# Attention of a two-layer decoder: three of four query tiles computed in quarters between the heads, the sample scores as one more unit of the rotation, the output projection begun inside it

## The reference

```
def sink_attention(q, k, v, dist, valid, sinks, rel_bias):
    ...
    s = jnp.einsum('nqgrd,nkgd->ngrqk', q, k, ...) * ATTN_SCALE + bias
    s = jnp.where(valid, s, NEG_INF)
    m = jnp.maximum(jnp.max(s, axis=-1, keepdims=True), sink)
    p = jnp.exp(s - m)
    probs = p / (jnp.sum(p, axis=-1, keepdims=True) + jnp.exp(sink - m))
    return jnp.einsum('ngrqk,nkgd->nqgrd', probs.astype(v.dtype), v)

q = (rmsnorm(x, g_mix[l]) @ w_q[j])
o = window_attn_prompt(...) or window_attn_sample(...)
x = x + o @ w_o[j]
h = rmsnorm(x, g_ffn[l])
x = x + moe_swiglu(h, ...)
```

## Time and profile before

| | |
|---|---|
| median of 3 runs | 1666.62 us (1665.63 to 1669.33) |
| the profiled execution, its own time | 1667.54 us |
| its span | 1665.8 us |
| PE busy | 1541.1 us, 93% |
| PEld busy | 1311.5 us |
| DVE busy | 1228.1 us, 74% |
| ACT busy | 962.3 us, 58% |
| chain that ended last, by engine | PE 89%, DVE 6%, ACT 2% |

### The profile page before, as it was taken

How to read it: one execution, slowest core, us unless ns; L and a number is a source line. 1 busy time by engine, 2 the same in 40 slices (tenths; PEclk the granted TensorE clock), 3 DMA queues, 4 the chain that set the end, 5 groups by cost and what they waited for, 6 DMA issues and landing times.

```text
span 1665.8 us, 22245 instructions
## 1 busy us (share of the span) xinstructions
PE 1541.1 (93%) x8280; PEld 1311.5 (79%) x8281; DVE 1228.1 (74%) x1137; ACT 962.3 (58%) x904; POOL 120.0 (7%) x141
## 2 busy tenths in 40 slices
PE   2589989999889879999998999998999999999995
PEld 1578989999777768888887888887888888888884
DVE  7843565553654257989887889887988988888984
ACT  3433443433454226777765776765776776776772
POOL 3970102000100000000000000000000000000000
PEclk9679989999975679999999999999999999999998
DMA  2004588445440025999987999997999998999980
GB/s 99 26 1 162 202 130 301 180 174 180 149 184 1 11 91 228 359 374 349 368 316 284 369 361 352 363 338 280 359 366 360 358 363 313 355 362 363 359 353 28
DMA packets 61933, 423.56 MB, mean 254 GB/s; under 512 B 8302, under 2 KB 8454, under 8 KB 11665
## 3 DMA queue, kind: packets, MB, share of 16 engines
q1 hardware_dynamic: 58784, 412.37, 65.6%
q0 software_dynamic: 3056, 9.85, 3.0%
HBM read 415.31 MB, written 6.88 MB: 253 GB/s over the span
## 4 chain that ended last, share of the span: by engine, by line
PE 89%; DVE 6%; ACT 2%; issue 2%; DMA 0%; SPq 0%; DVEq 0%; ACTq 0%
PE ps L1633 25%; PE ps L1635 24%; PE ps L1634 24%; PE ps L1828 2%; PE ps L1841 1%; PE ps L1463 1%; PE ps L1521 1%; PE ps L1552 1%; PE ps L1553 1%; PE ps L1854 1%; PE ps L1721 1%; PE ps L1748 1%; PE ps L1499 1%; PE ps L1710 1%; ACT WH L635 1%
## 5 line engine op out<-in xcount | busy, mean ns | idle before, releaser
L1138 DVE TENSOR_TENSOR WL<-raw,WH 128x2048 fp32r<-128x2048 f32 x387 | 885.8, 2292 | 211.7 <-ACT WH L635 208.2
L635 ACT CAST WH<-raw 128x2048 fp32r<-128x2048 f32 x387 | 738.4, 1910 | 201.0 <-PE ps L1635 201.0
L1633 PE MATMUL ps<-WH,XEH 128*128 128x512 f32 x896 | 361.8, 404 | 10.5 <-DVE WL L1138 9.0
L1635 PE MATMUL ps<-WH,XEL 128*128 128x512 f32 x896 | 353.1, 394 | 0.0
L1634 PE MATMUL ps<-WL,XEH 128*128 128x512 f32 x896 | 351.6, 392 | 0.0
L1633 PEld LDWEIGHTS ps<-WH,XEH 128*128 128x128 f32 x896 | 169.4, 189 | 45.6 <-DVE WL L1138 9.4
L1635 PEld LDWEIGHTS ps<-WH,XEL 128*128 128x128 f32 x896 | 169.4, 189 | 42.8
L1634 PEld LDWEIGHTS ps<-WL,XEH 128*128 128x128 f32 x896 | 169.4, 189 | 35.3
L1633 PE MATMUL ps<-WH,AFH 128*128 128x512 f32 x448 | 178.2, 398 | 0.0
L1634 PE MATMUL ps<-WL,AFH 128*128 128x512 f32 x448 | 176.8, 395 | 0.0
L1635 PE MATMUL ps<-WH,AFL 128*128 128x512 f32 x448 | 176.8, 395 | 0.0
(11 more groups left out here) (358 smaller groups left out, 1845.3 us busy)
## 6 DMA issues: line engine op xcount, KB each, us to landing
raw<-in_we SPq DMA_DIRECT2D x336, 1024.0 KB, 5.5
raw<-in_wd SPq DMA_DIRECT2D x51, 1024.0 KB, 4.9
bias_rows<-SC POOLq DMA_DIRECT2D x1, 3072.0 KB, 37.0
BIAS<-bias_rows POOLq DMA_DIRECT2D x16, 128.0 KB, 8.8
U<-in_xu SPq DMA_DIRECT2D x1, 1280.0 KB, 7.1
X<-in_xT SPq DMA_DIRECT2D x1, 1056.0 KB, 9.9
out_yT<-XN SPq DMA_DIRECT2D x2, 528.0 KB, 2.7
out_ks<-KCT POOLq DMA_DIRECT2D x1, 1024.0 KB, 7.7
```

What stands on the lines that cost most here:

```text
L635: a.copy(WH[tile[2] % SPLIT][:, :], raw[slot_][:, :]).then_inc(sem("hi_made"), 1)
L1138: v.tensor_tensor(WL[tile[2] % SPLIT][:, :], raw[tile[2] % RING][:, :], hi_, ALU.subtract)\
L1633: t_.matmul(out, sh, mh, start=first, stop=False)
L1635: return t_.matmul(out, sl, mh, start=False, stop=last)
```

## The change

1. **Queries.** Only the first query tile is computed before the heads. The other three are computed in quarters: in each of the first twelve steps PE does, behind `score(u)`, 12 of a tile's 48 products (`q_quarter`). They use one bank, number 7. ACT empties it in steps 2, 4, 6, 8, 10 and 12 (`q_out`), as the first thing of the step.
2. **Splitting in halves.** `hi` and `lo` work on halves of a tile everywhere in the kernel, 1024 columns each; `split` counts halves. In the experts PE waits for a tile's first half, and for the second before the second half of its products. In the dense tiles it waits for both.
3. **Splitting inside the heads.** `hi` and `lo` of the tiles O0, O0 + 1 and O0 + 2 stand at the end of steps 4, 8 and 12.
4. **Sample tokens.** `score_decoded` and the transposition are gone. ACT puts the sample queries into a block matrix `QS` in step 12 (`new_queries`, eight small copies); PE multiplies it with the cached keys in 16 products of 128 columns. This is a unit of the rotation: the order is heads 0 to 12, the sample unit, heads 13 to 15 (`UNITS`, index u), 17 steps. Its products with the values are `mix` of that unit, in step 16.
5. **Output projection.** The first output tile is computed in parts between the last `mix` and `turn` (`o_first`); `OTH` and `OTL` got a place of their own, and the banks of the output tiles are listed in `O_BANK`.

```diff
+UNITS = list(range(13)) + [NH] + [13, 14, 15]
...
-                a.copy(WH[tile[2] % SPLIT][:, :], raw[slot_][:, :]).then_inc(sem("hi_made"), 1)
+                for i in range(2):
+                    cols = slice(i * TILE // 2, (i + 1) * TILE // 2)
+                    a.copy(WH[tile[2] % SPLIT][:, cols], raw[slot_][:, cols]).then_inc(sem("hi_made"), 1)
...
+            for u in range(NU):
+                if u in (2, 6, 10):
+                    q_out(u // 2 + 1)
+                if u in (4, 8, 12):
+                    q_out(u // 2 + 1)
+                if u == 12:
+                    new_queries()
+                exps(u)
+                if u >= 1 and UNITS[u - 1] < NH:
+                    second_block(u - 1)
+                if u >= 2:
+                    turned_out(u - 2)
+                if u in (4, 8, 12):
+                    hi(dense(Q0 + SPLIT + u // 4))
...
+            for u in range(NU):
+
+                scores(u)
+                if u:
+                    probs(u - 1)
+                if u >= 5:
+                    unit_out(u - 4)
+                if u in (4, 8, 12):
...
+            probs(NU - 1)
+            for u in range(NU - 4, NU):
+                unit_out(u)
...
+            def q_quarter(n, s):
+
+                i, k0 = s // 2, 4 * (s % 2)
+                if s == 0:
+                    arrived(dense(n))
+                if s % 2 == 0:
+                    pe.wait_ge(sem("q_ready"), 2 * (n - Q0) + i)
...
+            for u in range(NU):
+                score(u)
+                if u < 12:
+                    q_quarter(Q0 + 1 + u // 4, u % 4)
+                if u >= 3:
+                    mix(u - 3)
+                if u >= 2:
+                    turn(u - 2)
+            arrived(dense(O0))
+            mix(NU - 3)
+            turn(NU - 2)
+            pe.wait_ge(sem("os_ready"), 1)
+            pe.wait_ge(sem("s_read"), NU)
+            o_first(0, range(6))
+            mix(NU - 2)
+            turn(NU - 1)
+            o_first(0, (6,))
+            o_first(1, range(7))
+            mix(NU - 1)
+            o_first(0, (7,))
+            o_first(1, (7,)).then_inc(used, 1)
```

More of the change, by code:

```diff
@@ L270, in tokens @@
             return P if t < 2 else TS
+        heads_upto = lambda u: sum(h < NH for h in UNITS[:u + 1])
+        exps_upto = lambda u: sum(3 if h < NH else 2 for h in UNITS[:u + 1])
         loaded = [sem(f"tile_loaded_{i}") for i in range(RING)]
@@ L1200, in _ @@
             scale_and_split(XQ, G_MIX1, sem("xq_ready"), 12, XQL, XQH)
-            for n in range(KV0, O0):
+            for n in range(KV0, Q0 + 1):
                 lo(dense(n + SPLIT))
@@ L1637, in arrived, with pair @@
             def arrived(tile):
[L1639 removed]
+                pe.wait_ge(split, at(pe, tile, 1, 2))
                 return WH[tile[2] % SPLIT], WL[tile[2] % SPLIT]
[L1642 removed]
+            def pair(tile, rhs, wait=None, n_split=None, banks=None):
                 w = arrived(tile)
@@ L1651, in pair @@
                         cols = slice((2 * k + i) * P, (2 * k + i + 1) * P)
-                        mm = passes(ps[:, 2 * (tile[2] % 2) + i, 0:NT], [x[:, cols] for x in w],
+                        bank = banks[i] if banks else 2 * (tile[2] % 2) + i
+                        mm = passes(ps[:, bank, 0:NT], [x[:, cols] for x in w],
                                     [x[:, k, :] for x in rhs], k == 0, k == KC - 1)
@@ L1752, in _ @@
-            pe.wait_ge(sem("kc_ready"), 1)
-            for h in range(NH):
-                score(h)
-                if h >= 3:
-                    mix(h - 3)
-                if h:
-                    score_decoded(h - 1)
-                if h >= 2:
-                    turn(h - 2)
-            mix(NH - 3)
-            turn(NH - 2)
-            score_decoded(NH - 1)
-            turn(NH - 1)
-            mix(NH - 2)
-            pe.wait_ge(sem("st_ready"), 2)
-            t_.transpose(ps[:, S_BANK[NH % 3], 0:P], STS[:, :], ident[:, :]).then_inc(sem("s_made"), 1)
@@ L1768, in _ @@
-            mix(NH - 1)
-            turn(NH)
-            pe.wait_ge(sem("pt_ready"), NH + 1)
-            pe.wait_ge(sem("cache_loaded"), 16 * (TS + 1))
-            pe.wait_ge(sem("new_v_loaded"), 16)
-            for b in range(TS):
-                for g in range(NKV):
-                    rows = slice(64 * (g % 2), 64 * (g % 2) + 64)
-                    out = ps[rows, 6, 0:KC * TS].rearrange("p (c b) -> p c b", c=KC)
-                    mm = t_.matmul(out[:, 4 * (g // 2):4 * (g // 2) + 4, b], VC[:, b, g * HD:(g + 1) * HD],
-                                   PTT[:, 0, b * NH + g * R:b * NH + g * R + R], start=True, stop=True)
@@ new lines, in _, with score @@
+            pe.wait_ge(sem("v_ready"), 3)
+            def score(u):
+                h, bank = UNITS[u], S_BANK[u % 3]
+                if u >= 3:
+                    pe.wait_ge(sem("s_read"), u - 2)
+                if h < NH:
+                    c, rows = h // 2, slice(64 * (h % 2), 64 * (h % 2) + 64)
+                    pe.wait_ge(sem("q_ready"), c + 1)
+                    kv = KT[rows, c // 4, :]
+                    t_.matmul(ps[:, bank, 0:W], QT[rows, c, 0:W], kv[:, 0:W], start=True, stop=True)
+                    t_.matmul(ps[:, bank, W:3 * W], QT[rows, c, W:TP], kv[:, 0:2 * W], start=True, stop=True)\
+                        .then_inc(sem("s_made"), 1)
+                    return
+                pe.wait_ge(sem("kc_ready"), 1)
+                pe.wait_ge(sem("qs_ready"), 8)
+                for b in range(TS):
+                    for i in range(2):
+                        mm = t_.matmul(ps[32 * (b // 2):32 * (b // 2) + 32, bank, 0:W], QS[:, b, i, :], KCT[:, b, i, :],
+                                       start=(b % 2 == 0 and i == 0), stop=(b % 2 == 1 and i == 1))
+                mm.then_inc(sem("s_made"), 1)
```

273 lines of the change are left out of this document (140 added, 133 removed).

## The result

The changed kernel takes 1638.03 us (median of 4 runs, 1636.41 to 1638.48) where the kernel before takes 1667.26 beside it (4 runs, 1665.63 to 1669.33). The ratio is 0.9822, with a 95% interval of 0.9806 to 0.9838: 29 us less. I had forecast 1645.

What follows compares the result with a forecast made beforehand. Heads taken as bound by PE's products at half clock, experts by PE. First residual add moves from 574.98 to 553, 22 us off 1667.54: 1645.5, or 1644.6 against the median; forecast 1645, range 1630 to 1660.

Steps and rivals of the forecast that it cites:

- Outside the heads, nothing: Norm, router and experts after the first residual add keep their order and, like the halves there, cost and gain nothing.
- DVE's cover: Experts: halves add 0.6 us per four tiles on DVE, covered by the 1.16 us DVE stood.
- The first steps and the clock: Start of heads: PE waits 3.6 us, the clock falls and returns within a quartered step; first `lo` ends at 482.8.
- The cycle of four steps: Quartered head steps: 18.3 us a cycle, 20.3 if the gap drops the clock; two cycles 40.6, ending at 523.4.
- The tail: Sample unit to first residual add: 27 us at full clock, 39 at half; 32 taken, from 521 to 553.
- PE begins the sample unit at about 521: End of step 12: PE starts the sample unit there; adding 32 us gives the first residual add at 553.
- The sum: First query copy to first residual add: its end moves from 574.98 to 553, 22 us gained.
- the clock stays at 0.50: Rival, heads: only slow products, no idle PE to fill; 2 us gained, 1665.5, no change; chance 0.10.
- Clock up: Rival, heads: gaps stay small, 1.00 is held, PE's work binds; 1630 us; chance 0.15 for 1626 to 1638.
- DVE bound in the experts: Rival, `lo` in 56 gate-up groups: halves make DVE the bound; 1681 us at 0.45 us more a tile; slower 0.08.
- more gap: Rival, even steps: a further wait of 1.5 us, six times, 9 us less gained, 1654; chance 0.12.

Runs made afterwards that it cites:

- the version with the early copy: Changed kernel with ACT's copy of a query tile's first chunk, which frees bank 7, one step earlier (steps 1, 5, 9): 1627.46 us, ratio 0.9761.

## Why the prediction was right, and where it was off

**Outside the heads, nothing.** Right as to DVE's cover, though not by its numbers: two halves in a row take 2.36 us and not 2.44, and DVE's idle time in a group of four tiles had to cover 0.2 to 0.3 us and not 0.6. What I put at nothing came out at 2.4 us less: 1.5 in the stretch of norm and router, 1.8 in the experts, 0.9 more at the end. I had written that PE hardly waits in the experts. It waits 9.0 us at the two turns of the loop, and 8.9 in the changed kernel; three waits of 0.3 us are gone. So about 1.0 of the 1.8 us are waits, and the rest stays open.

**The first steps and the clock.** The gap was forecast at 3.6 us until 466.8; it was 2.63, until 466.44. The clock fell at 467.6 and was back at 474.4: 6.8 us, where I had it come back within a quartered step at half clock, 6.5. The first `lo` was to end at 482.8 and ended at 483.1 (480.74 + 2.36).

**The cycle of four steps.** 20.3 with a fall, 18.3 without: measured 19.98 and 18.26. The mechanism is right, and the sums are closer than their terms. In the second cycle the four terms (to the quarter of step 10, to the end of score 11, to that of score 12, to the end of `lo`) were forecast at 4.0, 3.4, 3.4 and 7.5 with the signals and came out at 3.7, 3.9, 3.8 and 6.9; that they cancel to 0.1 is luck. PE's gap was 2.95 and not 4, as PE was ready 0.8 us behind the end of `lo` (503.9) and not ahead of it. That the fall comes in both cycles was wrong, so the third `lo` ended at 521.3 and not at 523.4. The clock fell after the gaps of 2.63 and 2.95 us and held through the one of 2.95 before 506.82. By the rule of the Trainium skill that I had weighed, "TensorE: Matmul & The Clock Gate", section "HAM oscillation — how this bites in real kernels", each gap costs the clock; the trace agrees at two of three. The kernel described in that section of the Trainium skill waits some 3 to 5 us each time, longer than these gaps; within the wait of 3.2 us before 523.64, and within that of the version with the early copy, the clock fell.

**The tail.** Forecast at 32 us, measured 32.15 (515.88 to 548.03). Inside, two terms were off in opposite ways: the 32 block products took 2.43 us at full clock where I had 3.5 (at half clock I had 7.0; the version with the block matrices alone took 3.99, most of it at 0.50), and the wait of 3.2 us with half clock from 522 to 539 was more than the middle between my bounds; that the tail as a whole came out right is luck. What failed is where the tail begins, "PE begins the sample unit at about 521": PE took it up 5.5 us before the end of the third `lo`, not 2.4, since it runs ahead of DVE's list in step 12 as the kernel's order allows.

**The sum.** 22 us forecast for the stretch, 26.95 measured. Of the 5 us, 2.1 are the earlier end of the third `lo`, for the most part the fall that did not come in the second cycle, and 3.1 the earlier start of the sample unit. The 2.4 us behind the stretch come on top: 29. The bounds of the forecast were added up wrongly: by its own terms they are 482.8 + 36.6 - 2.4 + 27 - 3.1 = 541 and 482.8 + 46 - 2.4 + 39 = 565, not 538 and 561. Neither end was reached.

**Where the gain comes from.** Here the prediction misleads. Its rival "the clock stays at 0.50" gave 1665.5, no change, as though the gain hung on the clock. The version without quarters has 0.50 for 40 us of heads and takes 1641.9. The rival kept the quarters (12 x 2.64 us at half clock) and 39 us of tail, and no version has quarters and a clock that stays low, so it stands untested; but it did not say what the block matrices are worth by themselves. They are worth 19.5 us: 9.5 as 0.95 us leaves each of ten steps, 4.83 to 3.88, and 10 at the end, where the sample unit's chain no longer stands alone and the clock was up for some 10 us. The rest: about 3 the halves, 2.5 the early output, 4 the quarters, by the versions that leave one out or have one alone, the last two near the noise. The parts are not independent: without the halves the changed kernel is at 1645.1, and the halves alone bring 3, not 7.

**The other rivals.** "Clock up" (1630) was wrong for this order, and near for the one that frees bank 7 early: 1627.5, with 1.00 from 460 to 510 but 0.50 from 511.8 to 528.8. "DVE bound in the experts" and "more gap" did not come.

## What to carry to other kernels

When work is put inside a software pipeline, look up for each engine's list what each new instruction stands behind: a copy of 0.36 us, placed one step later than its data allowed, cost 10 us, and a subtraction queued ahead of the scores cost 7. Before crediting a gain to the clock, make a version that leaves it low, and look whether it does so everywhere: here the one with 40 us of heads at half clock had 25 of the 29 us, but its clock had come up in the tail. And work with no reader can be faster than none where the clock is low (3 us here), but it can also cost: filling the gap in the tail came out level with moving the wait away (1621.6 and 1620.3), and mixing such work into the small products lost 6 us.

## What was not expected of the hardware

- PE busy 40.00 of 40.00 us left the granted clock at 0.50 (steps of transposes, scores and values); 12 products of 256 columns in each step brought it to 1.00 and held it for 55 us.
- Of two gaps of the same length, 2.95 us, one brought the clock down and the other did not. Ahead of the first PE had run at 1.00 for 9.5 us, ahead of the second for 12.4. I know of no row that tells them apart.
- Two subtractions of 1024 columns in a row took DVE 2.36 us, where one takes 1.22 and one of 2048 columns 2.29: cutting a long instruction in two cost 0.07 us and not the 0.15 of a straight line through two sizes.
- The block products, with 32 output rows and 128 columns, took 0.076 us a record (32 in 2.43 us), less than half of what the score records of 128 columns take at full clock. Two of those are 0.33 us in the version without quarters:

```profile
528.38 0.48 PE L1759 MATMUL ps<-KT,QT 64*128 64x128 f32 x2
528.71 0.59 PE L1760 MATMUL ps<-KT,QT 64*128 64x256 f32 x2
```
